# Single-pass products with constant tables in an attention stage, with SP split into a rounded part and the rest

## The reference, cut to what matters

```python
def stick_breaking_attention(q, k, v):        # A[t,s] = sigmoid(z_ts) prod_{s<j<t} (1 - sigmoid(z_tj)), s < t
    z = q k^T * 64 ** -0.5
    log_1m = where(s < t, log_sigmoid(-z), 0)
    rest = reverse cumulative sum of log_1m over s, without its own term
    wts = where(s < t, exp(log_sigmoid(z) + rest), 0)
    return wts @ v

def mla_attention(q_nope, q_rope, k_nope, k_rope, v):
    s = (q_nope k_nope^T + q_rope k_rope^T) * 96 ** -0.5
    return softmax(where(s' <= t, s, -inf)) @ v
```

## Time and profile before

| | us |
|---|---|
| median of three executions | 4022.08 |
| lowest, highest | 4013.43, 4032.09 |
| the profiled execution, its own time | 4017.63 |
| its span, from the first to the last instruction | 4015.8 |
| mean granted TensorE clock in it | 0.979 of 2.4 GHz |

### The profile page before, as it was taken

One profiled execution on the slowest core, in us unless ns is written; L12 is line 12 of the kernel. 1 busy time (PEld: TensorE's weight loads), 2 busy tenths in 40 slices (PEclk: granted clock), 3 DMA queues, 4 the chain that ended last, 5 costly groups with the idle time before them and its releaser, 6 DMA issues.

```text
span 4015.8 us, 70971 instructions
## 1 busy us (share of the span) xinstructions
PE 3828.5 (95%) x30814; PEld 3144.7 (78%) x30814; DVE 2085.2 (52%) x2908; ACT 1308.6 (33%) x1889; POOL 145.3 (4%) x195
## 2 busy tenths in 40 slices
PE   7998968989999999999989999999999988999998
PEld 5766868888868888888877688887888877688887
DVE  4977566755454445334755553354333755553335
ACT  4244233313333233222423522223222332532222
POOL 0000012230000000000000000000000000000000
PEclk8999979999999999999999999999999999999999
DMA  6213000023343223333102033323333201033331
GB/s 249 73 53 116 11 3 3 4 83 132 126 142 105 95 95 95 105 95 105 59 3 88 11 110 97 103 89 100 95 96 109 65 13 66 24 94 101 95 105 53
DMA packets 317735, 327.81 MB, mean 82 GB/s; under 512 B 8016, under 2 KB 241504, under 8 KB 316016
## 3 DMA queue, kind: packets, MB, share of 16 engines
q1 hardware_dynamic: 310064, 286.87, 21.9%
q0 software_dynamic: 7360, 36.40, 2.5%
HBM read 314.86 MB, written 8.39 MB: 80 GB/s over the span
## 4 chain that ended last, share of the span: by engine, by line
PE 84%; DVE 9%; ACT 3%; issue 2%; DMA 1%; POOL 0%; DVEq 0%; ACTq 0%; SPq 0%
PE psum L247 83%; DVE arena L301 2%; PE psum L254 2%; ACT arena L351 1%; DVE arena L312 1%; DVE ring L332 1%; DVE r L301 1%; DVE ring L301 1%; ACT r L351 1%; ACT ring L351 1%; DMA ring<-in_w_ada 0%; DVE arena L332 0%; DMA ring<-in_w_in 0%; DVE arena L316 0%; DVE ring L308 0%
## 5 line engine op out<-in xcount | busy, mean ns | idle before, releaser
L247 PE MATMUL psum<-r 128*128 128x512 f32 (+2 forms) x12912 | 2830.5, 380 | 31.4 <-DVE r L301 29.2
L247 PEld LDWEIGHTS psum<-r 128*128 128x128 f32 x12912 | 2334.6, 188 | 499.3 <-DVE r L301 30.4
L301 DVE TENSOR_TENSOR r<-ring,r 128x2048 fp32r<-128x2048 f32 (+1 forms) x259 | 573.2, 2213 | 309.9 <-ACT r L351 306.3
L351 ACT ACTIVATE r<-ring 128x2048 fp32r<-128x2048 f32 (+1 forms) x259 | 478.2, 1846 | 366.5 <-PE psum L247 310.5
L351 ACT ACTIVATE arena<-psum 128x512 f32<-128x512 f32 (+6 forms) x505 | 265.7, 527 | 978.1 <-PE psum L247 905.1
L247 PE MATMUL psum<-arena 64*64 64x64 f32 (+10 forms) x5922 | 453.7, 261 | 30.3 <-DVE arena L301 10.8
L247 PEld LDWEIGHTS psum<-arena 64*64 64x64 f32 (+5 forms) x5922 | 313.3, 151 | 154.7 <-issue 87.6
L301 DVE TENSOR_TENSOR arena<-arena,psum 128x512 f32<-128x512 f32 (+4 forms) x209 | 130.9, 626 | 569.6 <-PE psum L247 551.8
L247 PE MATMUL psum<-ring 64*64 64x64 f32 (+3 forms) x7792 | 291.0, 229 | 41.3 <-ACT ring L351 16.7
L247 PEld LDWEIGHTS psum<-ring 64*64 64x64 f32 (+2 forms) x7792 | 251.2, 139 | 64.7 <-issue 28.6
L351 ACT ACTIVATE r<-arena 128x512 fp32r<-128x512 f32 (+1 forms) x176 | 109.4, 622 | 503.0 <-DVE arena L301 500.8
(11 more groups left out here) (114 smaller groups left out, 1487.3 us busy)
## 6 DMA issues: line engine op xcount, KB each, us to landing
ring<-in_ffa_w_in SPq DMA_DIRECT2D x88, 512.0 KB, 4.7
ring<-in_ffb_w_in SPq DMA_DIRECT2D x88, 512.0 KB, 4.6
ring<-in_w_mlp SPq DMA_DIRECT2D x32, 1024.0 KB, 5.0
ring<-in_w_in SPq DMA_DIRECT2D x31, 1024.0 KB, 5.1
ring<-in_w_ada SPq DMA_DIRECT2D x24, 1024.0 KB, 5.0
ring<-in_mix_w_in SPq DMA_DIRECT2D x24, 1024.0 KB, 4.9
ring<-in_ffa_w_out SPq DMA_DIRECT2D x20, 1024.0 KB, 4.9
ring<-in_ffb_w_out SPq DMA_DIRECT2D x20, 1024.0 KB, 4.8
```

Source lines behind the costliest of these rows:

```text
L247: ins = self.raw.matmul(o, l, r, start=start, stop=stop, skip_group_check=True)
L301: self.done(self.raw and self.raw.tensor_tensor(o, a, b, f), keys)
L351: self.done(self.raw and self.raw.activation(o, i, f, scale=scale, bias=bias), keys)
```

## The change

A second set of names `K.R` is made for the constant tables: float32r views of the same memory. ScalarE converts the identity in place at the start (TensorE now waits for that copy), and four more tables in place once, after the delta rule of the first layer (`act_tables`). All other products with the identity keep reading it as float32.

`SP` is split. A new turn `p` follows the list above at four places. In it ScalarE writes the rounded part of each tile of `SP` (`SPhi`), and VectorE subtracts it from `SP` in place (`SPlo`). The rounded part of tile 0 lies in two new places of the ring, those of tiles 1 to 3 in the part of `SP` that no query uses. In `a` and `b` each product with `SP` becomes two, one for each part, and these, the masks there and the masks of the softmax scores take float32r operands. `a` waits for the last subtraction of its head.

```diff
+    cst = K.rounded(RING + 1024, 128 * len(names))
+    K.R = {k: cst[:, 128 * i:128 * i + 128] for i, k in enumerate(names)}
+    K.R["none"] = view(K.R["nUI128"][:, 127:128], [0, 128])
+    K.C["ident raw"], K.C["ident"] = K.C["ident"], K.R["ident"].bitcast(F32)
...
+    m.SPlo = [view(K.rounded(mk_h + 2048 * z, 2048), [512, 4], [1, 512]) for z in range(2)]
+    first = [K.rounded(SLOT * NSLOT + 6144 + 512 * z, 512) for z in range(2)]
+    lend(1024)
+    m.SPhi = [[first[z]] + [m.SPlo[z][:, 4 - s, 0:512 - 128 * s] for s in (1, 2, 3)] for z in range(2)]
...
+    a.wait_ge(*K.at("in", "ident"))
+    a.copy(K.R["ident"], K.C["ident raw"], ("ident r",))
...
+def act_tables(E, K):
+    a = ScalarLine(E, "sb")
+    a.wait_ge(*K.at("in", "consts again"))
+    for name in ("nUI128", "nLI128", "negLT", "negGE"):
+        a.copy(K.R[name], K.C[name], ("sb tables",))
...
-ATTENTION_TURNS = ("z0 e0 v0 z1 e1 v2 l0 m0 h0 l1 h1 h2 h3 a0 r0 m1 b0 r1 o0 z2 r2 e2 r3 l2 m2 r4 a1 r5 b1 r6 o1 z3 r7 e3 r8 l3 m3 r9 "
-         "a2 r10 b2 r11 o2 r12 a3 s0 r13 b3 r14 s1 r15 o3 r16 s2 r17 T s3 t").split()
+ATTENTION_TURNS = ("z0 e0 v0 z1 e1 v2 l0 m0 h0 p0 l1 h1 h2 h3 a0 r0 m1 b0 r1 p1 o0 z2 r2 e2 r3 l2 m2 r4 p2 a1 r5 b1 r6 o1 z3 r7 e3 "
+         "r8 l3 m3 r9 p3 a2 r10 b2 r11 o2 r12 a3 s0 r13 b3 r14 s1 r15 o3 r16 s2 r17 T s3 t").split()
...
-    SP, WT = m.SP[h % 2], m.eb[h % 2]
+    t.wait_ge(*K.at("sb tables"))
+    SP, WT = [m.SPhi[h % 2], [m.SPlo[h % 2][:, s, 128 * s:512] for s in range(4)]], m.eb[h % 2]
...
-        t.wait_ge(*K.at("sb sp", l, h))
+        t.wait_ge(*K.at("sb sp lo", l, h))
...
-            t.mm(o[:, 0:N], C["nLI128"], SP[:, s, lo:512], False, False)
+            for x in SP:
+                t.mm(o[:, 0:N], R["nLI128"], x[s], False, False)
             for j in range(s + 1, 4):
                 c = 128 * (j - s)
-                t.mm(o[:, c:N], C["none"], SP[:, j, 128 * j:512], False, False)
-            t.mm(o[:, 0:128], C["ident"], C["negGE"], False, True, ("sb w", l, h, s))
+                for x in SP:
+                    t.mm(o[:, c:N], R["none"], x[j], False, False)
+            t.mm(o[:, 0:128], R["ident"], R["negGE"], False, True, ("sb w", l, h, s))
...
+    elif kind == "p":
+        for s in range(4):
+            a.wait_ge(*K.at("sb sp", l, h, s))
+            a.copy(m.SPhi[h % 2][s], m.SP[h % 2][:, s, 128 * s:512], ("sb sp hi", l, h, s))
...
+    elif kind == "p":
+        for s in range(4):
+            lo = 128 * s
+            v.wait_ge(*K.at("sb sp hi", l, h, s))
+            v.tt(m.SPlo[h % 2][:, s, lo:512], SP[:, s, lo:512], m.SPhi[h % 2][s], SUB, ("sb sp lo", l, h))
...
-            t.mm(o[:, N - 128:N], C["ident"], C["negLT"], False, True, ("mla s", l, n))
+            t.mm(o[:, N - 128:N], R["ident"], R["negLT"], False, True, ("mla s", l, n))
...
-    E.wait_ge(*K.at("in", "ident"))
+    E.wait_ge(*K.at("ident r"))
...
         E.meet(f"delta rule done {l}")
+        if l == 0:
+            act_tables(E, K)
         act_sb_in(E, K, l)
```

More of the change, by code:

```diff
@@ L3625, in dve_sb_in @@
     E.ahead()
-ATTENTION_TURNS = ("z0 e0 v0 z1 e1 v2 l0 m0 h0 l1 h1 h2 h3 a0 r0 m1 b0 r1 o0 z2 r2 e2 r3 l2 m2 r4 a1 r5 b1 r6 o1 z3 r7 e3 r8 l3 m3 r9 "
-         "a2 r10 b2 r11 o2 r12 a3 s0 r13 b3 r14 s1 r15 o3 r16 s2 r17 T s3 t").split()
+ATTENTION_TURNS = ("z0 e0 v0 z1 e1 v2 l0 m0 h0 p0 l1 h1 h2 h3 a0 r0 m1 b0 r1 p1 o0 z2 r2 e2 r3 l2 m2 r4 p2 a1 r5 b1 r6 o1 z3 r7 e3 "
+         "r8 l3 m3 r9 p3 a2 r10 b2 r11 o2 r12 a3 s0 r13 b3 r14 s1 r15 o3 r16 s2 r17 T s3 t").split()
 def take_turns(sb, mla):
     for turn in ATTENTION_TURNS:
-        (sb if turn[0] in "zelmabosT" else mla)(turn[0], int(turn[1:] or 0))
+        (sb if turn[0] in "zelmpabosT" else mla)(turn[0], int(turn[1:] or 0))
 def pe_sb(E, K, l, kind, h):
-    t, m, C = TensorLine(E, "sb"), K.m, K.C
+    t, m, R = TensorLine(E, "sb"), K.m, K.R
     if kind == "T":
@@ L3721, in dve_sb @@
             v.tt(SP[:, s, lo:512], SP[:, s, lo:512], e[:, s, lo:512], ADD)
-            v.tt(SP[:, s, lo:lo + 128], SP[:, s, lo:lo + 128], K.C["US128"], MUL, ("sb sp", l, h))
+            v.tt(SP[:, s, lo:lo + 128], SP[:, s, lo:lo + 128], K.C["US128"], MUL, ("sb sp", l, h, s))
+    elif kind == "p":
[3 more added lines that the diff above has]
+            v.tt(m.SPlo[h % 2][:, s, lo:512], SP[:, s, lo:512], m.SPhi[h % 2][s], SUB, ("sb sp lo", l, h))
     elif kind == "o":
@@ L3757, in pe_mla @@
 def pe_mla(E, K, l, kind, n):
-    t, m, C = TensorLine(E, "mla"), K.m, K.C
+    t, m, R = TensorLine(E, "mla"), K.m, K.R
     ukv = view(m.ukv[:, 0, 0:], [1, 512])
```

## The result

The change makes the kernel slower. Eight executions of the changed kernel took 4061.85 us (median, 4039.89 to 4086.90), eight of the kernel before 4025.68 us (4013.43 to 4032.09): a ratio of 1.0089, 95% interval 1.0072 to 1.0106, or 36 us. The spread is new too: 47 us where it was 19. The profiled execution was the fastest of the eight, 4039.89 us with a span of 4037.7 us.

A forecast was written before the change was run, and what follows sets the result against it. TensorE bounds the kernel, nearly equalled by a VectorE/ScalarE chain early in attention. Waits outweigh TensorE's 19.0 us saving: 0.6 us more per layer, clock loss unchanged, +1 us; predicted 4023 us, range 4008 to 4040.

The forecast's parts named there:

- What TensorE loses: Attention: cheaper single-pass SP products and masks save TensorE 19.0 us in all, 1.57 us of it in each `a`.
- The turns `p`: Attention: each adds 2.0 us on ScalarE, 2.1 on VectorE; waits outweigh the saving, stage 0.6 us longer per layer.
- The clock: Attention of both layers: time lost to TensorE's lowered clock stays at 8.2 us in total, as before.
- The 14 us in which TensorE was to idle in each layer: Attention: TensorE idles some 14 us per layer instead of 4.2, and half clock costs nothing while it waits.
- The sign of being wrong that the prediction named: Attention profile: a stage below 95 us, or granted clock under 0.9 over the whole stage.
- Rival (b): Attention: longer gaps hold the clock down, eight slow stretches of 3.3 us instead of 8.2 us total; 4041 us, chance 0.15.
- Rival (a): Attention: TensorE stays the limit and the turns `p` find slack; up to 4003 us, chance 0.14.
- Rival (c): Attention: products with the new operands don't run single-pass, 35 us more work, partly covered; 4048 us, chance 0.03.
- 3.5 us in all: Attention: extra TensorE saving at the 32 SP products of 128 columns if the skill's pass count held; not adopted.
- The rest: Outside attention: table copies cost nothing (uncovered, under 2 us); the start's wait for the identity nothing (uncovered, 0.5).

The follow-up runs named there:

- filler of 64 rows: Changed kernel with one more FP32 product of equal width, on 64 rows, ahead of each score product in `a` and `b`, result overwritten: 4106.22 us.
- the one of 128 rows: Changed kernel with one more FP32 product of equal width, on 128 rows, ahead of each score product in `a` and `b`, result overwritten: 4052.60 us.

## Why the prediction was wrong

**What TensorE loses** was right in size. I took 1.57 us for `a`, so 4.5 us; the trace has 4.41. The kernel without the turns `p` comes out 16 us under before once half clock is taken off (10 to 22, as above), against 19.

**The turns `p`** are where I put them. ScalarE's four copies of `p0` take 2.14 us (2.0 expected) and VectorE's subtractions 2.28 (2.1):

```profile
2215.34 2.14 ACT L351 ACTIVATE r<-arena 128x512 fp32r<-128x512 f32 x4
```

```profile
2219.26 2.28 DVE L301 TENSOR_TENSOR r<-arena,r 128x512 fp32r<-128x512 f32 x4
```

`a0` waits for 2.86 us (2.7). What the waits cost in the end was overrated. I let them eat all of the 19 us and one more. The split with FP32 masks is 9 us slower with its turns than without (4034.1 against 4024.9, with 210 and 201 us at half clock), and the turns alone cost 14 us with 25 us more at half clock, some 10 of them the clock's. So 4 to 6 us are left for the waits, and that error stood on the other side: put right alone, it would have moved the forecast further down, away from the result.

**The clock** is the step that failed. "I take the same 8.2 us in the two layers as before", it said, with TensorE's waits as the only thing that could change it. In the first profile the mean clock of the two stages is 0.89 over 108 us and 0.69 over 123 us, which is 24 and 76 us at 1.2 GHz; before it was 0.98 and 0.94, 4 and 13 us. Over all executions it is 127 us more, or 51 us of time. The 14 us in which TensorE was to idle in each layer, and half clock to cost nothing, were 9 and 3. The sign of being wrong that the prediction named, a granted clock under 0.9 over the whole stage, is in both stages. Rival (b) had the direction and half the size (18 us more than the forecast, 4041; measured 36 more than before) and half the cause. It was right that the clock falls behind gaps, but it let each fall last as long as before (3.3 us of time, eight times), and the loss is in how long it lasts: 75 us in one piece. That doesn't come from the added gaps: the kernel with the turns and the old products has 202 us at half clock, the one with the new products and without the turns 296. I read the products only for their time. That TensorE's FP32 work, for which the change offered a cheaper form, was also what kept the clock up was in none of my cases, so the range ended at 4040.

**Rival (a)**, slack under the turns, was nearer for the waits than my own sum. **Rival (c)** is out: `a` is shorter by just the single-pass prices. `a3`'s 4.41 us fits the prices of the earlier trace rows to 0.1 us. The pass count of the Trainium skill (FP8 and Floating Point Precision, section TensorE Precision Notes) is not borne out at 128 columns here: by an estimate from it, `a3`'s four SP records and two masks of 128 columns would take 0.055 us each instead of 0.1135, and `a3` some 4.15 us. The "3.5 us in all" that the prediction gave for that count left out the 64 masks, another 3.7 us.

**The rest** was hidden, as said. The copies of the tables, with ScalarE idle on both sides of them, and the start of the kernel:

```profile
2143.22 1.34 ACT L351 ACTIVATE r<-arena 128x128 fp32r<-128x128 f32 x4 [7.25 <-DVE arena L301]
...
2149.24 0.23 ACT L351 ACTIVATE arena<-arena 128x32 f32<-128x32 f32 x1 [3.37 <-DVE arena L312]
```

```profile
8.18 3.59 PE L247 MATMUL psum<-ring,head 64*2 64x512 f32 x16 [8.18 <-ACT r L351]
12.16 1.04 PE L247 MATMUL psum<-ring,head 64*2 64x512 f32 x8 [0.39 <-DMA ring<-in_w_ada]
```

The first of them before:

```profile
7.50 3.31 PE L247 MATMUL psum<-ring,head 64*2 64x512 f32 x16 [7.50 <-DMA arena<-in_consts]
```

TensorE starts 0.7 us later (8.18 against 7.50) and waits 0.8 us less for the weights.

## What to carry to other kernels

Before you replace FP32 products by single-pass ones, look at what stands around them. In a stage of short products, products of 64 rows and transposes, the FP32 products may be what holds the clock, and a saving of some microseconds can cost tens. The sum of a change's durations at one clock is not a forecast in such a stage; compare the mean granted clock of its stretches, in several executions, and keep the long or many-pass products where the others use little of the array.

## What the runs showed of the hardware

TensorE can be busy without a gap for 75 us (changed kernel) and 125 us (filler of 64 rows) and stay at 1.2 GHz throughout; both stretches began behind a gap of 2.86 us, and behind the same gap the old products were back at full clock after 7 us. With everything else equal, 64 masks in two single-pass records instead of two FP32 records raised the time at half clock from 210 to 393 us, and the filler of 64 rows against the one of 128 rows from 239 to 369. The time of one kernel follows its clock at 0.3 to 0.5 us for each microsecond at half clock, which also explains most of the spread between the executions of one kernel.
